# Side work inside the projection products, and an attention that uses the values of the second kind as weights, two heads at a time

## What is computed

```
h = RMSNorm(x)                                   # 520 x 1024
q_d,k_d,v_d | q_s,k_s,v_s | q_idx,k_idx,w_idx | gate_d,gate_s = h @ W_in
y_d = DiffAttn(q_d,k_d,v_d) @ W_od               # 4 heads of two softmaxes each, p1 - lam*p2, values 128 wide, RMSNorm of each head
y_s = SparseAttn(q_s,k_s,v_s; index) @ W_os      # 8 heads, values 64 wide, only the 128 keys of highest index score per query
x = x + (sigmoid(gate_d)*y_d + sigmoid(gate_s)*y_s) @ W_out
x = x + MoE(RMSNorm(x))                          # 32 experts, two of them per token
```

## Time and profile before

| | |
|---|---|
| time, median of 3 runs (range) | 1251.58 us (1247.12 to 1252.23) |
| profiled execution: its own time | 1250.04 us |
| its span, first to last instruction | 1247.9 us |
| mean granted TensorE clock | 0.958 |
| TensorE matmul busy | 1064.7 us (85%) |
| VectorE busy | 454.3 us (36%) |
| ScalarE busy | 232.7 us (19%) |
| GpSimd busy | 263.3 us (21%) |
| transfers | 304.13 MB, mean 244 GB/s |

### The profile page before, as it was taken

One profiled execution on the slowest core, in us unless ns is written; L12 is line 12 of the kernel. 1 busy time (PEld: TensorE's weight loads), 2 busy tenths in 40 slices (PEclk: granted clock), 3 DMA queues, 4 the chain that ended last, 5 costly groups with the idle time before them and its releaser, 6 DMA issues. The chain is left out here.

```text
span 1247.9 us, 16077 instructions
## 1 busy us (share of the span) xinstructions
PE 1064.7 (85%) x6029; PEld 556.3 (45%) x6029; DVE 454.3 (36%) x1209; ACT 232.7 (19%) x505; POOL 263.3 (21%) x242
## 2 busy tenths in 40 slices
PE   4998889978998999997899969998878877787773
PEld 3554434434454555532256535544434444344442
DVE  4345888885464555322143423211111110111110
ACT  2112212110233333322004311111011011110100
POOL 1011100220453434200200012223222222222111
PEclk9999989989999999898999969999999999999997
DMA  5141122014564533679738549999999999999991
GB/s 182 41 149 33 54 85 93 27 68 164 175 219 134 187 103 102 222 254 332 242 131 343 178 179 401 403 394 392 406 407 405 402 398 401 400 407 405 405 384 40
DMA packets 77120, 304.13 MB, mean 244 GB/s; under 512 B 22402, under 2 KB 22402, under 8 KB 64754
## 3 DMA queue, kind: packets, MB, share of 16 engines
q1 hardware_dynamic: 61618, 273.47, 57.2%
q0 software_dynamic: 9824, 16.98, 4.8%
q10 hardware_dynamic: 5600, 12.65, 2.8%
HBM read 290.03 MB, written 29.66 MB: 256 GB/s over the span
## 5 line engine op out<-in xcount | busy, mean ns | idle before, releaser
L381 PE MATMUL p_z<-k_w,k_xT 128*128 128x512 f32 (+2 forms) x528 | 213.3, 560 | 0.6 <-PEq L148 0.6
L381 PEld LDWEIGHTS p_z<-k_w,k_xT 128*128 128x128 f32 (+1 forms) x528 | 94.8, 193 | 108.2 <-issue 106.7
L793 PE MATMUL a_G<-k_w,k_xT 128*128 128x512 f32 x256 | 130.3, 632 | 2.5 <-ACT k_x L851 2.5
L1938 DVE TENSOR_TENSOR e_den<-e_sig,e_G 128x256 f32<-128x256 f32 x32 | 13.5, 421 | 277.7 <-ACT e_sig L1843 277.7
L888 POOL TENSOR_TENSOR k_x<-k_x 128x512 f32<-128x512 f32 x64 | 80.4, 1269 | 109.8 <-DVE k_side L952 86.7
L1848 ACT ACTIVATE e_y<-e_Y,x_share 64x512 f32<-64x512 f32 x64 | 43.7, 684 | 314.8 <-PE e_Y L1751 305.9
L1969 POOL DMA_INDIRECT out_y_p<-e_y,x_table x32 | 45.0, 1407 | 199.4 <-ACT e_y L1848 154.8
L141 POOL DMA_INDIRECT k_rows<-token_rows,x_table x32 | 31.3, 978 | 187.4 <-PE e_TX L1733 162.1
L793 PEld LDWEIGHTS a_G<-k_w,k_xT 128*128 128x128 f32 x256 | 45.1, 197 | 49.2 <-issue 45.1
L1142 PE MATMUL g_ring<-k_w,k_oT 128*128 128x512 f32 x128 | 60.4, 618 | 0.0
L1943 DVE TENSOR_TENSOR e_a<-e_den,e_U 128x256 f32<-128x256 f32 x32 | 13.5, 421 | 126.5 <-PE e_U L1739 126.5
(11 more groups left out here) (343 smaller groups left out, 1474.5 us busy)
## 6 DMA issues: line engine op xcount, KB each, us to landing
k_w<-in_w_in SPq DMA_DIRECT2D x11, 2048.0 KB, 7.8
k_w<-in_w_gate SPq DMA_DIRECT2D x11, 2048.0 KB
k_w<-in_w_up SPq DMA_DIRECT2D x11, 2048.0 KB
k_xT<-in_w_down SPq DMA_DIRECT2D x11, 2048.0 KB
k_oT<-in_w_gate SPq DMA_DIRECT2D x11, 2048.0 KB
k_side<-in_w_up SPq DMA_DIRECT2D x11, 2048.0 KB
x_page<-in_w_down SPq DMA_DIRECT2D x11, 2048.0 KB
x_merged<-in_w_gate SPq DMA_DIRECT2D x10, 2048.0 KB
```

The source lines that it names most:

```text
L381: last = nc.tensor.matmul(z[u % 3][0:p, 0:WIDTH[k]], s.xT[:, j, 128 * i:128 * i + p], s.w[:, c % 2, j, 0:WIDTH[k]], start=j == 0, stop=j = ...
L793: last = nc.tensor.matmul(G[u % 2][:], s.xT[:, j, 128 * i:128 * i + 128], s.w[:, q % 2, j, :], start=j == 0, stop=j == KD - 1)
L1938: v.tensor_tensor(den[:], sig[:], G[j][:, 0:HW], ALU.mult).then_inc(chain, 1)
```

## The change

In `project` TensorE's side work moves between the matmuls of a product. The transposes of earlier units come after matmul 1 (and 4) of a later product, the sample pairs after matmuls 0, 2, 4 and 6 of unit 12, and three index scores after matmuls 2, 5 and 7 of each prompt unit from unit 15 on (8 units instead of 12). VectorE now does the side work of unit u ahead of `sums(u)` and `finish(u)`, mixed with rounds of `take8`. Where a unit has scores it takes 1 round (4 for values) instead of 2 (5), and the sample tiles take none at all. ScalarE's order follows.

In `attend_prompt` kind s no longer multiplies transposed probabilities (as weights) with 64 columns of values. The 64 value columns of a head are the weights, the transposed probabilities (128 columns) move, and two heads go to the lower and upper 64 partitions of one bank. The result comes out already transposed, so the 4 output transposes of each of the 4 tiles of kind s, the division of the 128x512 output and one copy (four times each) go away. In their place each of the 32 units of kind s gets a reciprocal on VectorE (`invert`) and a scaling of its probabilities in place on ScalarE (`divide`). `pT` has 4 buffers instead of 2.

```diff
+def turns(u):
+    i = u % TILES
+    at = [(1, u - 3), (4, u - 2)] if i == 0 else [(1, u - 2)] if i < NT else []
+    return [(j, v) for j, v in at if v >= 0 and is_turned(UNITS[v])]
...
-        extras = {IDX_FROM + 2 + n // 2: IDX_STEPS[n:n + 2] for n in range(0, len(IDX_STEPS), 2)}
+        PAIR_AT = {2 * n: n for n in range(PAIRS)}
+        EXTRA_AT = (2, 5, 7)
+        prompt_units = [u for u in range(SAMPLE_AT + 2, U) if UNITS[u][1] < NT]
+        extras = {prompt_units[n // 3]: IDX_STEPS[n:n + 3] for n in range(0, len(IDX_STEPS), 3)}
...
+                for j in range(KD):
+                    last = nc.tensor.matmul(z[u % 3][0:p, 0:WIDTH[k]], s.xT[:, j, 128 * i:128 * i + p],
+                                            s.w[:, c % 2, j, 0:WIDTH[k]], start=j == 0, stop=j == KD - 1)
+                    if j == KD - 1:
+                        last.then_inc(proj, 1)
+                    for at, v in turns(u):
+                        if at == j:
+                            turn(v)
...
+                    if u in extras and j in EXTRA_AT:
+                        index_scores(*extras[u][EXTRA_AT.index(j)])
...
+                room = 0 if i == NT else (1 if k in NORMED else 4) if u in extras else (2 if k in NORMED else 5)
...
-                for _ in range(0 if i == NT else 2 if k in NORMED else 5):
-                    if rounds:
+                    if room and rounds:
+                        room -= 1
                         take8(rounds.pop(0))
-            masks()
+                while room and rounds:
+                    room -= 1
+                    take8(rounds.pop(0))
+                if u == U - 1:
+                    masks()
+                sums(u)
+                if k in NORMED and i < NT and rounds:
+                    take8(rounds.pop(0))
+                finish(u)
...
-                w = W // (4 if kind == "d" else 8)
-                for b in range(t + 1):
-                    last = nc.tensor.matmul(O[g % 2][:, w * h:w * h + w], pT[:, q % 2, 128 * b:128 * b + 128],
-                                            s.v[KQV[kind][2]][:, b, w * h:w * h + w], start=b == 0, stop=b == t)
-                last.then_inc(pv_done, 1)
...
+                elif h % 2:
+                    if h == 1 and t:
+                        pe.wait_ge(s_out, t)
+                    j = h // 2
+                    for b in range(t + 1):
+                        for r in range(2):
+                            last = nc.tensor.matmul(O_s[64 * r:64 * r + 64, 128 * j:128 * j + 128], s.v["vs"][:, b, 128 * j + 64 * r:128 * j + 64 * r + 64],
+                                                    pT[:, (q - 1 + r) % 4, 128 * b:128 * b + 128], start=b == 0, stop=b == t)
+                            if b == t:
+                                last.then_inc(pv_done, 1)
...
+            def divide(n):
+
+                t, m = A_UNITS[n][0], singles_before(n + 1)
+                act.wait_ge(inv_ready, m)
+                nc.scalar.mul(prob[:, n % 4, 0:128 * (t + 1)], prob[:, n % 4, 0:128 * (t + 1)], inv[:, n:n + 1]).then_inc(p_scaled, 1)
...
+            def invert(n):
+
+                dve.wait_ge(p_ready, n + 1)
+                nc.vector.reciprocal(inv[:, n:n + 1], sums[:, n:n + 1]).then_inc(inv_ready, 1)
...
+            def output_s(t):
+
+                dve.wait_ge(pv_done, last_job[t, "s"] + 1)
+                nc.vector.tensor_copy(s.oT["s"][:, :, 128 * t:128 * t + 128], O_s[:].rearrange("p (j q) -> p j q", j=NB)).then_inc(s_out, 1)
```

More of the change, by code:

```diff
@@ new lines, in pair @@
+            def pair(step):
+                if step < PAIRS:
+                    bank = take_bank()
+                    for n in range(NPAGE):
+                        last = nc.tensor.transpose(bank[:, 128 * n:128 * n + 128],
+                                                   pages_i[:, n, 2 * step:2 * step + 2, :].rearrange("p b d -> p (b d)"), s.ident[:])
+                    last.then_inc(x_ready, 1)
+                b = step - 1
+                if b >= 0:
+                    pe.wait_ge(kTi_ready, b + 1)
+                    last = nc.tensor.matmul(ss[:], qblk[:, 64 * b:64 * b + 64], kTi[:, b % 2, :], start=b == 0, stop=b == PAIRS - 1)
+                    last.then_inc(ss_ready, 1)
@@ new lines, in new_keys, with sample_scores @@
+            def new_keys():
+                bank = take_bank()
+                pe.wait_ge(newk_ready, 2)
+                for b in range(PAIRS):
+                    nc.tensor.matmul(bank[0:64, 0:1], qblk[:, 64 * b:64 * b + 64], newk[:, b:b + 1], start=b == 0, stop=b == PAIRS - 1)
+                pe.wait_ge(wi_ready, TILES)
+                nc.tensor.matmul(bank[0:64, 8:16], s.c[0:NS, C_E:C_ET], wi[0:NS, NT, :], start=True, stop=True).then_inc(x_ready, 1)
+            def sample_scores():
+                pe.wait_ge(samp, 3)
+                bank = take_bank()
+                nc.tensor.matmul(bank[0:NS, :], ew[:], relu_s[:, 0:PAST], start=True, stop=True).then_inc(x_ready, 1)
+                bank = take_bank()
+                nc.tensor.matmul(bank[0:NS, 0:1], ew[:], relu_s[:, PAST:PAST + 1], start=True, stop=True).then_inc(x_ready, 1)
@@ L423, in _ @@
             ns = nt = nx = nz = 0
-            for u in range(U + 2):
+            for u in range(U):
                 if u == 2:
@@ L427, in _ @@
                     nc.scalar.activation(lexp, lsum, ACT.Exp).then_inc(lam_exp, 1)
[L428 to L445 removed]
+                for _, v in turns(u):
                     k, i = UNITS[v]
@@ L487, in _ @@
                     nc.scalar.activation(relu_s[:, PAST:PAST + 1], xs[PAIRS % 2][0:64, 0:1], ACT.Relu, scale=DH ** -0.5).then_inc(samp, 1)
+                if UNITS[u][1] == NT and UNITS[u][0] != "kw":
+                    act.wait_ge(proj, u + 1)
+                    if u >= TILES:
+                        act.wait_ge(y_ready, u - TILES + 1)
+                    for g in range(NB):
+                        nc.scalar.copy(zs[:, 128 * g:128 * g + 128], z[u % 3][32 * g:32 * g + NS, 0:128]).then_inc(zs_ready, 1)
+                    nz += NB
+                    act.wait_ge(zs_ready, nz)
+                if UNITS[u][0] in NORMED:
+                    p = ROWS[UNITS[u][1]]
+                    act.wait_ge(proj, u + 1)
+                    if ns >= 2:
+                        act.wait_ge(ms_ready, ns - 1)
+                    nc.scalar.activation(sq[0:p, ns % 2, :], (z[u % 3][0:p, :] if p > NS else zs[:]), ACT.Square).then_inc(squared, 1)
+                    ns += 1
         @block.gpsimd
@@ L703, in attend_prompt @@
         pairs_before = lambda n: sum(k == "d" and h % 2 for _, k, h in A_UNITS[:n])
-        last_job = {g: max(q for q, j in enumerate(JOBS) if 2 * j[0] + (j[1] == "s") == g) for g in range(2 * NT)}
+        singles_before = lambda n: sum(k == "s" for _, k, _ in A_UNITS[:n])
+        last_job = {(t, kind): max(q for q, j in enumerate(JOBS) if j[:2] == (t, kind)) for t in range(NT) for kind in "ds"}
         jobs_upto = lambda n: sum(j[3] <= n - LAG for j in JOBS)
@@ L866, in _ @@
                                          accum_out=sums[:, n:n + 1]).then_inc(p_ready, 1)
+                if 1 <= n <= UN and A_UNITS[n - 1][1] == "s":
+                    divide(n - 1)
                 for u in [u for u in range(len(GATES)) if GATE_DONE[u] == n - 1]:
@@ L979, in _ @@
             key_sum(len(KEYS) - 1)
-            for g in [g for g in range(2 * NT) if last_job[g] > JN - 3]:
-                output(g)
-            for g in [g for g in range(2 * NT) if last_job[g] > JN - 5]:
-                output_turned(g)
+            output_s(NT - 1)
 SLOTS_A = len(PASSES) * NT
```

237 lines of the change are left out of this document (93 added, 144 removed).

## The result

| | before | after |
|---|---|---|
| time, median (range), 19 runs each | 1251.01 us (1246.40 to 1256.32) | 1255.97 us (1250.06 to 1263.05) |
| ratio after/before, 95% interval | | 1.0043 [1.0028, 1.0059] |
| profiled execution: own time, span | 1250.04, 1247.9 us | 1258.29, 1256.5 us |

The change made the kernel 0.43% slower, 5.4 us by the ratio; 1242.5 was predicted. The prediction's mechanism for the attention holds. Its sum for the projections is wrong in sign.

The account below looks back on a forecast made before the run. VectorE was taken to bound the projections after 111.2 us and TensorE the attention. Gains of 2.8 (projections) + 3.1 (value products) + 1.3 (transposes) + 1.0 (end) = 8.2 us gave 1242.5 us, range 1236 to 1250.

Parts of the forecast that it names:

- What bounds the kernel: Whole kernel: TensorE sets the attention, VectorE the projections after 111.2 us; a microsecond gained before 519 us counts at the end.
- The beginning of the projections: Sample pairs at unit 12 gain about 1 us, earlier `turn` of qi's tiles costs about as much; counted as nothing.
- these 10 us: End of projections: TensorE ends its last product near 297 us, VectorE near 307.5, which covers TensorE's new waits.
- The exposed rounds: Projections, VectorE: only 12 of 64 selection rounds hidden in GpSimd's holes instead of 16, 7.7 us more work.
- The waits of the stretch: Projections after the change: VectorE waits about 2.1 us at kd's first unit and 1.2 us for scores.
- 13.8 us: Projections from 111.2 us: all VectorE's waits before the change; less 7.7 and 3.3, the stage ends 2.8 us earlier.
- that don't count as long as VectorE is behind: Projections: TensorE waits 1 to 4 us in about twelve places, priced at nothing while VectorE is behind.
- The sign "VectorE waiting over 5 us for products or scores before vd": Projections: listed among the observations that would show the prediction wrong.
- The third rival: Projections gain nothing because VectorE waits as often in new places; time 1245, chance 0.2.
- The slower rival that I priced, ScalarE's queue: Attention kind s: late divisions delay `copy`, each unit pays 0.63 us; time 1262, chance 0.05.
- The value products, transposes and end: Attention: paired value products gain 3.1 us, three dropped output transposes 1.3, shorter path before `merge` 1.0.

Follow-up runs that it names:

- kw_late: Kernel after, but transposes of the sample tiles of qi and kw stand behind matmul 7 instead of matmul 1; 1253.60 us, ratio to before 1.0007.
- all3: Kernel after with sample-tile transposes behind matmul 7, index scores paired over twelve units, and a round in the sample tiles' hole; 1243.00 us, ratio to before 0.9941.
- best: all3 with the samples' index part also moved behind the products of units 12 and 13; 1243.08 us, ratio to before 0.9925.
- sample_behind: Kernel after, but the samples' index part stands behind the products of units 12 and 13, as before; 1254.41 us, ratio to before 1.0033.
- nt_round: Kernel after, but VectorE again takes a selection round in GpSimd's hole of the sample tiles; 1250.57 us, ratio to before 0.9991.
- same_half: Kernel before, with heads reordered so both matmuls of an index pair lie in the same half of the array's rows; 1254.96 us, ratio to before 1.0020.
- two_each: Kernel after, but its 24 index scores stand as 12 pairs, each behind one unit's whole product; 1251.88 us, ratio to before 0.9997.
- heads_apart: Kernel after, but value products of two kind-s heads run one head after the other instead of alternating by block; 1258.18 us, ratio to before 1.0050.
- pairs: Kernel after, but four index scores in each of six units, two behind matmul 2 and two behind matmul 6; 1259.15 us, ratio to before 1.0073.
- proj_only: `project` of the kernel after with `attend_prompt` of the kernel before; 1261.96 us, ratio to before 1.0067.

## Why the prediction was wrong

**What bounds the kernel.** Right. The projections end on VectorE (8.6 us of waiting for TensorE, then the last mask), and the attention is TensorE's. A microsecond before 519 us did count at the end: attention 5.3 us shorter, total 5.9 shorter.

**The beginning of the projections.** This is the first step that failed: "The sample pairs gain about 1 us at unit 12 and the earlier `turn` of qi's tiles costs about as much, which I count as nothing." It was +5.1 us. I priced the earlier transposes only where VectorE was behind anyway and used the cover of "these 10 us" for the whole stage, while before 111 us there is no cover: VectorE waits for TensorE there. What is late next when the one transpose of kw waits was not asked. kw_late shows 1.9 us of it in the stretch's start. The remaining 3.2 are not in one place. From the start of product 12 to the end of the small product of unit 14 TensorE needs 26.2 us in all3 (83.84 to 110.05) and 25.2 in the kernel before (82.68 to 107.89): 1 us more and not 1 less. And the side work inside products 12 and 13 now stands ahead of their ends, so the squares come later by it. VectorE's timeline of all3 shows it:

```profile
98.62 0.69 DVE L549 TENSOR_REDUCE p_ms<-p_sq 128x8 f32<-128x512 f32 x1 [5.94 <-ACT p_sq L514]
...
108.92 0.69 DVE L549 TENSOR_REDUCE p_ms<-p_sq 128x8 f32<-128x512 f32 x1 [3.73 <-ACT p_sq L514]
```

The kernel before had one wait of 6.49 us there. Moving the samples' part back gave 0.9 us (best) to 1.4 us (sample_behind) of the 3.2. The starts of the stretch of one code spread by 2 us, so this is a direction more than a size. The rest is read from the traces and not tested.

**The exposed rounds.** "7.7 us more work" was counted rightly: the waits in GpSimd's holes grew by 7.5 us (13.0 to 20.5). Giving back the samples' hole returned 6 us of it in the total (nt_round).

**The waits of the stretch.** This is the second step that failed: "For score waits I add 1.2 us". They were 6.0 us, and the wait at kd 2.6 instead of 2.1, together 5.3 more than forecast. The stretch came out at 203.3 us against a forecast of 196.5. Small waits that I priced at nothing add 2.0 us, and gaps between instructions most of the rest. In the other direction, the sum "13.8 us" of VectorE's waits was wrong: the view that it was taken from adds up to 15.8, so 2.0 us more went away. Where the clock fell behind the 2.50 us wait, the same stretch took 208.3 us, with 11.4 us of score waits. The prediction had waits inside a product only as ones "that don't count as long as VectorE is behind". The sign "VectorE waiting over 5 us for products or scores before vd" came true with 8.6 us.

The cause is in a price that I never wrote down. I took a single index score at half of a pair, 0.42 us, where the timeline now has 0.84. The pair of the kernel before lay in both halves of the array's rows and ran at once, which same_half proves by taking it away (1.48 us). So TensorE had up to 10 us more to do exactly in the units that became light for VectorE: it was busy without a gap from 170 to 210 us. The cover of 10 us that the prediction relied on exists at the end of the stage (8.6 us), where kind vd is full of rounds, and not in these units. two_each, which takes the 10 us away, brings the score waits of kind vs from 4.5 to 2.1 us and leaves the one at kd's first unit. The row for it was in the trace of before, L389 with 64 rows of weights in pairs. The prediction counted on two tiles at once in the attention and did not look for the same thing among the scores, which the diff takes apart. The Trainium skill, TensorEngine Tiling (Array Packing), Key Properties, says that different tiles can load weights and multiply in parallel. Both same_half and heads_apart agree, and add that it takes rows that stand close in the queue: four rows of one tile ahead of four of the other still ran in the time of alternating ones, six and eight did not.

With the kw transpose, the scores and the samples' hole put right (all3) the stretch is 195.7 us, the attention starts at 310.5, and the median is 1243.0. That it lies so near the forecast of 196.5 and 1242.5 is luck: all3 has also given back 6 us of rounds that the forecast counted as lost, and two_each, which has not, took 200.8.

**The third rival** ("VectorE waits as often in new places") had the right mechanism and stopped at no gain. The slower rival that I priced, ScalarE's queue, did not happen: TensorE waits for `copy` once, 0.8 us at the last pair.

**The value products, transposes and end.** Right in the sum and its parts: 3.1 + 1.3 + 1.0 = 5.4 us forecast, 5.3 measured. A pair of heads at tile 3 saves 1.80 - 1.12 = 0.68 us (0.62 forecast). Between the output transposes of kind d, tile 2 to 3 and tile 3 to `merge`, 54.62 and 22.72 us became 52.87 and 20.75. TensorE's rows of the kernel after for these:

```profile
449.17 0.66 PE L822 MATMUL a_T<-k_c,a_on 128*128 128x128 f32 x4 [1.03 <-DVE a_on L982]
...
502.04 0.66 PE L822 MATMUL a_T<-k_c,a_on 128*128 128x128 f32 x4 [0.81 <-DVE a_on L982]
```

## What to carry to other kernels

When a diff splits or moves small matmuls, look first at whether they were running in pairs in different tiles of the array, and price the single one by its own rows. A cover belongs to a stretch: work put inside a product is free only where the consumer of that product is behind, and each wait inside it delays that consumer too (pairs: 9.2 us of such waits). If two engines are both near the limit, relieve them together: each repair alone gave 0.36 to 0.52%, and the three together 1.0%. And before two profiles of different kernels are compared, look whether the clock fell behind the same waits: here one such place moved a stage by 5 us between executions of the same code.

## What the runs showed of the hardware

- Two float32 matmuls with 64 rows of weights in different halves of the array take 0.85 us for both at width 384 if they stand directly behind each other, 0.84 us for one alone, and 1.48 us for two in the same half.
- Float32 rows of 128 columns against 64 columns of weights start 0.054 us apart when they alternate between two column tiles. With two or four rows of one tile ahead of as many of the other the time is the same (0.37 and 0.60 us for 4 and 8 rows). With six and eight ahead each row more costs 0.11 to 0.12 us. With 128 columns of weights and 64 moving it was 0.105.
- A wait of TensorE of 2 to 2.5 us is sometimes followed by rows at the 1.2 GHz level and sometimes not, in the same code: behind the 2.50 us wait for `p_xs` six rows took 2.77 us in after and 5.42 in proj_only, and 5.35 in nt_round. In the attention the 2.05 us wait for `k_x` was followed by a slow stretch in some executions (after) and not in others (two_each, all3); with the same value products they took 203.1 to 203.3 and 200.3 to 201.0 us. What decides it stays open.
